# Attention layer of a four-layer diffusion trunk: where the query and key norms, the value turns and the key turns stand among the in-projection's panels

## The reference

```python
def na_project(h, w_qkv, q_norm, k_norm):
    q, k, v = jnp.split(h @ w_qkv, 3, axis=-1)        # 16 heads of 64
    return rms_norm(heads(q), q_norm), rms_norm(heads(k), k_norm), heads(v)

# context tokens: softmax(q k^T / 8) v over the 128 context tokens; k and v are outputs too
# latent tokens:  softmax over [window of 8 x 16 neighbours with a learned bias, 128 cached context keys]
s_loc = einsum(q_blk, k_blk) * scale + bias           # masked outside the window
s_ctx = einsum(q_blk, k_ctx) * scale
p = softmax(concatenate([s_loc, s_ctx]))
o = p[local] @ v_blk + p[context] @ v_ctx
out = merge_heads(o) @ w_out
```

## Time and profile before

| | |
|---|---|
| median of 3 runs | 2327.2 us |
| the runs | 2324.89 to 2328.65 us |
| profiled execution, span from first to last instruction | 2325.0 us |
| time around that span | none is given; the lowest run is 2324.89 us |
| PE busy | 2225.4 us, 96% |
| DVE busy | 481.9 us, 21% |
| ACT busy | 391.6 us, 17% |
| mean granted TensorE clock | 0.983 |
| DMA | 550.93 MB, mean 237 GB/s |

### The profile page before, as it was taken

The page is one execution under the profiler, slowest core; times in us unless marked ns, Lnnn a source line. Parts: engine busy times, 40 slices in busy tenths (PEclk is TensorE's granted clock), DMA queues, the critical chain, the costliest instruction groups (busy, mean ns, idle before and its releaser), DMA issues.

```text
span 2325.0 us, 44307 instructions
## 1 busy us (share of the span) xinstructions
PE 2225.4 (96%) x19787; PEld 1657.2 (71%) x19787; DVE 481.9 (21%) x1352; ACT 391.6 (17%) x795; POOL 66.9 (3%) x109
## 2 busy tenths in 40 slices
PE   6999999999999999999998999999998989999998
PEld 4776667888888756646676578888887877466465
DVE  2234432100121400000212320002335423000002
ACT  1133223100010100000113220001143331000001
POOL 4000001000000000000000000000000000000000
PEclk8999999999999999999999899999999999999999
DMA  8977789743346499999774696413440047999992
GB/s 330 265 251 287 287 313 295 229 151 112 119 153 217 159 375 387 383 378 378 284 233 172 229 263 189 145 37 109 145 141 11 12 158 251 383 387 381 380 381 118
DMA packets 355911, 550.93 MB, mean 237 GB/s; under 512 B 11280, under 2 KB 311184, under 8 KB 343232
## 3 DMA queue, kind: packets, MB, share of 16 engines
q1 hardware_dynamic: 344352, 525.31, 65.1%
q0 software_dynamic: 5840, 18.11, 3.0%
q10 hardware_dynamic: 5536, 4.73, 0.6%
HBM read 537.64 MB, written 14.93 MB: 238 GB/s over the span
## 4 chain that ended last, share of the span: by engine, by line
PE 78%; SPq 10%; DVE 5%; ACT 2%; DMA 2%; issue 2%; ACTq 0%; DVEq 0%
PE ps L643 76%; SPq L483 7%; SPq L487 3%; ACT ring L1451 2%; DMA ring<-in_moe_w_down 1%; DVE ring L2003 1%; ACT work L1451 1%; DVE ring L2021 0%; DVE work L1862 0%; DVE ring L2026 0%; DVE ring L2011 0%; DMA ring<-in_ada_w 0%; PE ps L1147 0%; PE ps L1041 0%; DVE ring L2029 0%
## 5 line engine op out<-in xcount | busy, mean ns | idle before, releaser
L643 PE MATMUL ps<-hT,ring 128*128 128x256 f32 x3200 | 713.4, 382 | 3.4 <-DVE hT L1872 3.2
L643 PE MATMUL ps<-ring,work 128*32 128x384 f32 (+7 forms) x8008 | 692.0, 436 | 21.8 <-DMA ring<-in_moe_w_gu 5.1
L643 PEld LDWEIGHTS ps<-hT,ring 128*128 128x128 f32 x3200 | 608.6, 191 | 112.9 <-issue 12.2
L643 PEld LDWEIGHTS ps<-ring,work 128*32 128x32 f32 (+2 forms) x8008 | 390.9, 114 | 301.6 <-issue 178.4
L1451 ACT ACTIVATE work<-ps 128x256 f32<-128x256 f32 (+6 forms) x220 | 100.5, 467 | 1330.0 <-PE ps L643 1151.2
L643 PE MATMUL ps<-work,ring 128*128 128x256 f32 (+1 forms) x1344 | 283.9, 370 | 2.0 <-DVE work L2107 1.5
L643 PEld LDWEIGHTS ps<-work,ring 128*128 128x128 f32 (+1 forms) x1344 | 238.1, 185 | 36.8 <-DVE work L2088 1.9
L643 PEld LDWEIGHTS ps<-ring 64*64 64x64 f32 x4192 | 159.6, 138 | 59.6 <-ACT ring L1451 24.2
L643 PE MATMUL ps<-ring 64*64 64x64 f32 (+1 forms) x4192 | 181.6, 229 | 20.2 <-ACT ring L1451 7.2
L1451 ACT ACTIVATE ring<-ps 128x512 f32<-128x512 f32 (+3 forms) x208 | 101.6, 491 | 340.7 <-PE ps L643 329.6
L643 PE MATMUL ps<-work 128*128 128x128 f32 (+2 forms) x736 | 106.3, 295 | 3.8 <-DVE work L2208 3.7
(11 more groups left out here) (260 smaller groups left out, 934.7 us busy)
## 6 DMA issues: line engine op xcount, KB each, us to landing
ring<-in_moe_w_gu SPq DMA_DIRECT2D x96, 1536.0 KB, 16.0
ring<-in_ada_w SPq DMA_DIRECT2D x96, 1024.0 KB, 6.8
ring<-in_moe_w_down SPq DMA_DIRECT2D x48, 1536.0 KB, 16.4
ring<-in_ff_w_gu SPq DMA_DIRECT2D x88, 512.0 KB, 6.0
ring<-in_dn_w_in SPq DMA_DIRECT2D x32, 1024.0 KB, 5.5
ring<-in_moe_w_gu SPq DMA_DIRECT2D x32, 1024.0 KB, 9.2
ring<-in_ff_w_down SPq DMA_DIRECT2D x44, 512.0 KB, 6.9
ring<-in_moe_w_down SPq DMA_DIRECT2D x32, 512.0 KB, 11.7
```

The costliest lines, as they stand in the source:

```text
L643: return pe.matmul(out, lhsT, rhs, start=start, stop=stop, **kw)
```

## The change

The counts of matmuls, transposes, copies, squares, Ln, Exp and multiplications stay as they are. Moved are:

- The eight `sums`: `sums(w - 1)` now stands right behind the ada panel of step w, for w = 1 to 8. ScalarE squares each query or key panel right after its copy, and works Ln and Exp of the panel before in the same step. The table load ahead of the chain goes.
- The value turns: a group is now two chunks of both token groups, that is one value panel, and waits for that panel's copy alone. Groups 0, 1 and 2 stand behind panels 9, 10 and 11, group 3 at the end.
- The context keys' turn stands behind panel 10, the keys' two turns behind panels 10 and 11, `ada_turn` behind panel 9. Keys are turned through banks 2 and 3, the ada panels of this stretch are summed in bank 6 and turned through bank 7.
- VectorE's order follows. The bias addition, which was waited out on VectorE itself, now counts a semaphore (`d_bias`) that PE awaits before the first scores. The values' copy writes a 3-D pattern (two token groups of 256 features).
- GpSimd waits for all four value copies instead of two before it stores the context values.

```diff
@@ pool queue @@
-            po.wait_ge(d_vt, VT0[2] + 2)
+            po.wait_ge(d_vt, VT0[2] + 4)
...
@@ -985,39 +986,53 @@
 
             def attention(l):
                 u = PLAN.first[l]["in"]
+
+                def ctx_turned():
+                    pe.wait_ge(ctx_in, 32)
+                    pe.wait_ge(d_ar, ada_turned[0])
+                    for m in range(2):
+                        for c in range(4):
+                            ins = pe.transpose(ps[:, 6 + m, c * P:(c + 1) * P],
+                                               kctok[:, (4 * m + c) * P:(4 * m + c + 1) * P], ident)
+                        ins.then_inc(p_ct, 1)
+
+                def v_turned(n):
+                    pe.wait_ge(a_pj, PJ0[l] + 9 + n)
+                    if n >= 2:
+                        pe.wait_ge(d_vt, VT0[l] + n - 1)
+                    for c in range(4):
+                        g, ch = c // 2, 2 * n + c % 2
+                        ins = pe.transpose(ps[:, 4 + n % 2, c * P:(c + 1) * P],
+                                           mixT[:, ch, g * P:(g + 1) * P], ident)
+                    ins.then_inc(p_vt, 1)
+
+                def k_turned(m):
+                    pe.wait_ge(d_l2, L20[l] + 7 + m)
+                    for c in range(4):
+                        ins = pe.transpose(ps[:, 2 + m, c * P:(c + 1) * P], kT[:, 4 * m + c, 0:P], ident)
+                    ins.then_inc(p_kt, 1)
+
                 for w in range(12):
                     if w >= 2:
                         pe.wait_ge(a_pj, PJ0[l] + w - 1)
                     project(u[w], w % 2, hT, 2 * l if w == 0 else None)
                     if 1 <= w <= NA_IN:
-                        ada(2, 3, ROWS512(l))
-                ada_turn(3, ROWS512(l))
-                pe.wait_ge(ctx_in, 32)
-                for m in range(2):
-                    for c in range(4):
-                        ins = pe.transpose(ps[:, 6 + m, c * P:(c + 1) * P],
-                                           kctok[:, (4 * m + c) * P:(4 * m + c + 1) * P], ident)
-                    ins.then_inc(p_ct, 1)
-                pe.wait_ge(a_pj, PJ0[l] + 12)
-                for m in range(4):
-                    if m >= 2:
-                        pe.wait_ge(d_vt, VT0[l] + m - 1)
-                    for c in range(4):
-                        ch, g = 4 * (m % 2) + c, m // 2
-                        ins = pe.transpose(ps[:, 4 + m % 2, c * P:(c + 1) * P],
-                                           mixT[:, ch, g * P:(g + 1) * P], ident)
-                    ins.then_inc(p_vt, 1)
-                pe.wait_ge(d_ar, ada_turned[0])
-                for w in range(8):
-                    sums(l, w, 2 + w % 2, blk64)
-                pe.wait_ge(d_vt, VT0[l] + 4)
-                pe.wait_ge(d_l2, L20[l] + 8)
-                for m in range(2):
-                    for c in range(4):
-                        ins = pe.transpose(ps[:, 4 + m, c * P:(c + 1) * P], kT[:, 4 * m + c, 0:P], ident)
-                    ins.then_inc(p_kt, 1)
+                        ada(6, 7, ROWS512(l))
+                        sums(l, w - 1, 2 + (w - 1) % 2, blk64)
+                    elif w == 9:
+                        ada_turn(7, ROWS512(l))
+                        v_turned(0)
+                    elif w == 10:
+                        ctx_turned()
+                        v_turned(1)
+                        k_turned(0)
+                    elif w == 11:
+                        v_turned(2)
+                        k_turned(1)
+                v_turned(3)
                 pe.wait_ge(d_ct, 2)
                 pe.wait_ge(d_kt, KT0[l] + 2)
+                pe.wait_ge(d_bias, 1)
                 pe.wait_ge(d_ar, ada_turned[0])
 
                 def scores(j):
@@ -1602,8 +1617,20 @@
                 for w in range(12):
                     act.wait_ge(unit_done, u[w] + 1)
                     f(dest[w], ps[:, w % 2, :], ACT.Copy).then_inc(a_pj, 1)
-                groups(l, [pair(qT, w) for w in range(4)] + [pair(kT, w) for w in range(4)], 0, 1.0 / HD,
-                       lambda w: act.wait_ge(a_pj, PJ0[l] + 12) if w == 0 else None)
+                    if w < 8:
+                        act.wait_ge(a_pj, PJ0[l] + w + 1)
+                        if w >= 2:
+                            act.wait_ge(p_l2, L20[l] + w - 1)
+                        f(SQ(l, w % 2), dest[w], ACT.Square).then_inc(a_l2sq, 1)
+                    if 1 <= w <= 8:
+                        v = w - 1
+                        act.wait_ge(p_l2, L20[l] + v + 1)
+                        if v >= 2:
+                            act.wait_ge(d_l2, L20[l] + v - 1)
+                        f(RS(l, v % 2), ps[:, 2 + v % 2, :], ACT.Ln, scale=1.0 / HD, bias=eps[:, 0:1]) \
+                            .then_inc(a_l2n, 1)
+                        act.wait_ge(a_l2n, L20[l] + v + 1)
+                        f(RS(l, v % 2), RS(l, v % 2), ACT.Exp, scale=-0.5).then_inc(a_l2r, 1)
 
                 def expo(j):
                     p = j % 2
@@ -2108,25 +2135,39 @@
 
             def attention(l):
 
-                dve.wait_ge(bias_in, 64)
-                link(tt(na_bias, na_bias, cst[:, None, C_NAM:C_NAM + P].to_broadcast([P, NH, P]), ALU.add))
-                ada_rows(2, ROWS512(l))
-                modulation(3)
-                for m in range(2):
-                    dve.wait_ge(p_ct, m + 1)
-                    cp(kctxT[:, 4 * m:4 * m + 4, :].rearrange("p c n -> p (c n)"), ps[:, 6 + m, :]).then_inc(d_ct, 1)
-                for m in range(4):
-                    dve.wait_ge(p_vt, VT0[l] + m + 1)
-                    cp(na_vtok[:, m // 2, 512 * (m % 2):512 * (m % 2) + 512], ps[:, 4 + m % 2, :]).then_inc(d_vt, 1)
                 link(ts(sv(GQ, 2)[:, 1:2], par[:, 6, 0:1], sv(GQ, 2)[:, 0:1], None, ALU.mult))
-                for w in range(8):
+
+                def normed(w):
                     t = pair(qT if w < 4 else kT, w % 4)
                     dve.wait_ge(a_l2r, L20[l] + w + 1)
                     stt(t, t, sv(GQ, 2)[:, 1:2] if w < 4 else par[:, 6, 1:2], RS(l, w % 2),
                         ALU.mult, ALU.mult).then_inc(d_l2, 1)
+
+                def v_turned(n):
+                    dve.wait_ge(p_vt, VT0[l] + n + 1)
+                    cp(na_vtok[:, :, 256 * n:256 * n + 256],
+                       ps[:, 4 + n % 2, :].rearrange("p (g n) -> p g n", g=2)).then_inc(d_vt, 1)
+
+                def k_turned(m):
+                    dve.wait_ge(p_kt, KT0[l] + m + 1)
+                    cp(ktok_na[:, 512 * m:512 * m + 512], ps[:, 2 + m, :]).then_inc(d_kt, 1)
+
+                dve.wait_ge(bias_in, 64)
+                tt(na_bias, na_bias, cst[:, None, C_NAM:C_NAM + P].to_broadcast([P, NH, P]), ALU.add).then_inc(d_bias, 1)
+                for w in range(7):
+                    normed(w)
+                ada_rows(6, ROWS512(l))
+                normed(7)
+                modulation(7)
+                v_turned(0)
                 for m in range(2):
-                    dve.wait_ge(p_kt, KT0[l] + m + 1)
-                    cp(ktok_na[:, 512 * m:512 * m + 512], ps[:, 4 + m, :]).then_inc(d_kt, 1)
+                    dve.wait_ge(p_ct, m + 1)
+                    cp(kctxT[:, 4 * m:4 * m + 4, :].rearrange("p c n -> p (c n)"), ps[:, 6 + m, :]).then_inc(d_ct, 1)
+                v_turned(1)
+                k_turned(0)
+                v_turned(2)
+                k_turned(1)
+                v_turned(3)
 
                 def highest(j):
                     p = j % 2
```

More of the change, by code:

```diff
@@ L285, in trunk @@
         d_z = sem("d_z")
+        d_bias = sem("d_bias")
         d_gate, d_fin, d_nx = sem("d_gate"), sem("d_fin"), sem("d_nx")
```

## The result

The changed kernel takes 2312.15 us (median of 4 runs, 2310.8 to 2314.93) against 2327.93 us; the ratio is 0.9941, interval 0.9926 to 0.9955. (The ratios on record are not quotients of the two medians; here that would be 0.9932, within the interval.) Measured once more in another set of runs it took 2310.46 us against 2327.81 us, 0.9931 (0.9915 to 0.9948). The profiled execution has a span of 2310.2 us and a device time of 2312.23 us, so 2.0 us lie around the span; that is what the prediction carried over as 2.2 us between span and median.

The account below looks back on a forecast made before the run. TensorE was taken to bound the kernel, in the chain of waits for 78% of the span. Holes 9.8 us (21.43 - 9.5 - 2.1) plus clock 4.3 gave 14.1 us saved, so 2313.1 us; range 2307.5 to 2318.5.

Parts of the forecast that it names:

- Sums into the panels, 6.9 us, and transposes, 2.6 us: Attention layer's panels: eight sums at 0.86 us and 24 moved transposes lengthen them by 9.5 us.
- one sign that the prediction named for being wrong: In the panels: a sum starting more than 0.9 us ahead of the next panel would show a term wrong.
- the worked step of 8.8 us: One panel step on TensorE: panel 7.0, ada panel 0.95 and sum 0.86 us, 8.8 us together.
- No waits inside the panels: TensorE never waits for ScalarE, VectorE or weights within the twelve panels; cost 0.
- The cover: Ahead of the norm multiplications: the bias addition on VectorE could end 25 us later before costing anything.
- The tail, 2.1 us: Last panel to first scores: 2.1 us, decided by VectorE's copy of the second key turn; range 1.8 to 2.8.
- The clock, 4.3 us: First scores to first turned probabilities: full clock instead of a low stretch, 9.3 us instead of 13.64, 4.3 less.
- The rule against it: Behind the last panel: transpose-mode does not count as PE-busy in the same way, so the gain would stay near 9.8 us.
- the rival: First scores: the clock falls anyway, gain 9.8 us only, 2317.4 us; chance 0.17 shared with one low stretch more.
- What is behind is unchanged: Behind the attention layer all work starts earlier by the same amount; the 14 us shift at 1293 remains at the end.
- a rival with 5 us either way: Later holes: one low stretch less, 2308 us, chance 0.13; one more, 2318 us, within 0.17 shared with clock falling anyway.
- Faster by 0.2% at 0.94: Whole run: chance 0.94 of measuring below 2322.5 us, faster by more than the 0.2% (4.7 us) a measurement can tell.

Follow-up runs that it names:

- the fillers: Kernel before the change, nothing moved, matmuls nobody reads added in TensorE's holes among the sums and ahead of the first scores; 2321.91 us against 2325.83, ratio 0.9987.
- norms alone: Against the kernel before, only the norms (sums, square, Ln, Exp) moved among the panels, all transposes left behind the twelfth; 2319.18 us against 2325.83, ratio 0.9976.
- turns alone: Against the kernel before, only value, context-key and modulation turns moved among the panels, norms left behind the twelfth; 2327.52 us against 2325.83, ratio 1.0005.

## Why the prediction was right

The time, 2312.15 us, lies 1 us from the 2313.1 predicted, and the three terms of the forecast came about as it says. The last microseconds are luck: the layer gained 2.7 us more than forecast, and 2.0 us were given back outside it.

- *Sums into the panels, 6.9 us, and transposes, 2.6 us.* The panels grew by 9.50 us. A step went from 8.08 to 8.94 us, 0.86 for the sum, the number of layer 3's row. But its neighbours are not quite the same, as an ada panel stands ahead of it, and one sign that the prediction named for being wrong did appear: the sums start 0.97 us ahead of the next panel, more than 0.9. The panel behind a sum then takes 7.00 us up to its ada panel instead of 7.10, so the step grows by 0.86 all the same. The same seam makes the worked step of 8.8 us a little short.
- *No waits inside the panels.* There are none; TensorE is busy 101.99 of 102 us. The cover was larger than I worked out (40 us of lateness, not 25).
- *The tail, 2.1 us.* 2.02, decided by VectorE's copy of the second key turn as forecast (1267.33 + 0.68, scores at 1268.11). The row of the scores names no releaser; but with that copy delayed the hole grew by 5.04 us, and the scores came 5.05 us later behind the last panel. The unknown copy pattern costs the same as the plain one.
- *The clock, 4.3 us.* 4.20, and the fillers show that it is the holes' doing and a term of its own. The rule against it does not hold for these transposes. One argument against the rival was wrong: that it took 15 us of sparse sums and two waits to bring the clock down. With the norms alone it fell after holes of 2.9 us in all. The changed kernel stayed at 1.00 with its one hole of 0.52; how near it is to falling is not shown.
- *What is behind is unchanged.* By the sign named for it, yes: the first turned probabilities come 15.0 us earlier and the end 14.8. In between it is not unchanged: 2.7 us less among the heads, where a low stretch went and another came, and 2.9 us more behind the layer. The prediction had a stretch that goes, moves or comes as a rival with 5 us either way; in this layer one went and one came.
- *Faster by 0.2% at 0.94.* The whole interval of the ratio, 0.45 to 0.74% faster, lies beyond that bound.

What was weak: the gain's parts were worked from one execution, while two executions of one program can lie 10 us apart. The medians of four runs hid this; it was luck as much as arithmetic that the time fell within 1 us.

## What to carry to other kernels

A chain of short steps between engines (square, sum, Ln, Exp, scale), worked after a long dense stage, costs its latency once per round; spread over the stage's panels, one round per panel, it costs only TensorE's own share. Here 9.5 us in the panels and 2.0 behind them stand for 21.4. Look first for which chain decides a tail: moving the turns alone bought nothing; after the norms had gone they bought 4.8 us. And price the clock separately from the holes: what follows a sparse stretch can run slow (here 4.2 us), and this part can be measured alone by filling the holes with matmuls that nobody reads.

## What the runs showed of the hardware

- 96 float32 transposes, 10.6 us with nothing else on TensorE, were worked at a granted clock of 1.00, and what followed too.
- The clock also fell after holes of only 0.4, 0.7, 0.8 and 1.0 us within 8 us (norms alone), about 2.5 us after the last of them, while TensorE was busy.
- Ten profiles, of nine kernels, have the holes of 1.95 and 3.11 us among the heads. A low clock followed the shorter in seven and the longer in seven, not always the same seven: before, turns alone and transposes only behind the shorter; the changed kernel (twice) and the filled one only behind the longer; the other four behind both.
- Two executions of one program can differ by 9.6 us of span, 7.7 of them time at the low clock.
